# A hybrid-mixer and mixture-of-experts trunk: queue order in the merge, tile-by-tile second half of the last projection, 2 MB expert loads and piecewise contraction waits

## The reference

```python
xn = rms_norm(h, norm1_g)
h = h + hybrid_mixer(xn, ...)          # four branches of width 256, then:
    branch = einsum('bskw,kwd->bskd', ys, branch_w)
    gates = sigmoid(xn @ merge_gate_w + merge_gate_b).reshape(bn, s, 4, 1024)
    merged = sum(gates * branch, axis=2)
    return merged @ w_out
xn = rms_norm(h, norm2_g)
h = h + hier_moe(xn, ...)              # 4 groups x 8 experts, top-1 group, top-2 experts:
    h_e = silu(xb @ w1[e]) * (xb @ w3[e])     # w1, w3: 1024 x 512
    y_e = h_e @ w2[e]                         # w2: 512 x 1024
return rms_norm(h, final_norm_g)
```

## Time and profile before

| | |
|---|---|
| median of 3 runs | 2709.32 us (2708.64 to 2713.03) |
| profiled execution, its own time | 2708.18 us |
| its span | 2706.5 us |
| PE busy | 2394.8 us, 88% of the span |
| DVE, ACT, POOL busy | 1365.7, 1102.4, 656.5 us |
| merge | about 556 to 1716.5 us of the span |
| route | 1716.5 to about 1770 us |
| experts | about 1770 to 2650 us |

### The profile page before, as it was taken

One profiled execution on the slowest core, in us unless ns is written; L12 is line 12 of the kernel. 1 busy time (PEld: TensorE's weight loads), 2 busy tenths in 40 slices (PEclk: granted clock), 3 DMA queues, 4 the chain that ended last, 5 costly groups with the idle time before them and its releaser, 6 DMA issues. The chain is left out here.

```text
span 2706.5 us, 33463 instructions
## 1 busy us (share of the span) xinstructions
PE 2394.8 (88%) x11388; PEld 1875.1 (69%) x11389; DVE 1365.7 (50%) x1922; ACT 1102.4 (41%) x1380; POOL 656.5 (24%) x515
## 2 busy tenths in 40 slices
PE   6679679789989999899989999489999999999890
PEld 5567567568868888788878888366666666677670
DVE  6768464544444344434434443645555554556554
ACT  4423324123333333233323332246566665567653
POOL 4811001000000000000000000076555656547660
PEclk9889889899999999999999999689999999999995
DMA  8753546434354334533353332369878977889877
GB/s 252 272 193 126 210 147 230 128 87 128 97 177 138 119 98 148 171 125 97 113 177 114 97 99 91 146 225 302 276 240 271 306 260 259 263 285 346 287 258 271
DMA packets 360507, 516.29 MB, mean 191 GB/s; under 512 B 32668, under 2 KB 211104, under 8 KB 360416
## 3 DMA queue, kind: packets, MB, share of 16 engines
q1 hardware_dynamic: 343952, 458.17, 49.5%
q0 software_dynamic: 16464, 56.90, 8.3%
HBM read 430.33 MB, written 84.68 MB: 190 GB/s over the span
## 5 line engine op out<-in xcount | busy, mean ns | idle before, releaser
L1468 PE MATMUL mrgps<-xn_hi,w_hi 128*128 128x512 f32 x1024 | 402.3, 393 | 9.5 <-DVE w_lo L1566 9.5
L1468 PE MATMUL mrgps<-xn_lo,w_hi 128*128 128x512 f32 x1024 | 400.2, 391 | 0.0
L1468 PE MATMUL mrgps<-xn_hi,w_lo 128*128 128x512 f32 x1024 | 400.1, 391 | 0.0
L1902 POOL TENSOR_TENSOR w_lo<-w_raw,w_hi 128x1024 fp32r<-128x1024 f32 x128 | 326.4, 2753 | 0.4 <-ACT w_hi L1893 0.4
L1409 ACT ACTIVATE gt<-mrgps,mb 128x512 f32<-128x512 f32 x128 | 88.3, 690 | 505.7 <-PE mrgps L1468 505.7
L1704 POOL IOTA io_g<- 128x4 f32 x1 | 0.1, 144 | 1156.3 <-POOLq L1218 1156.3
L1897 DVE TENSOR_TENSOR w_lo<-w_raw,w_hi 128x2048 fp32r<-128x2048 f32 x125 | 280.5, 2304 | 0.1
L1582 DVE SCALAR_TENSOR_TENSOR tmp<-gt,mrgps 128x512 f32<-128x512 f32 x96 | 66.0, 688 | 389.4 <-PE mrgps L1468 389.4
L1888 ACT ACTIVATE w_hi<-w_raw 128x2048 fp32r<-128x2048 f32 x128 | 240.0, 1914 | 16.5 <-DMA w_raw<-in_expert_w_dram 16.4
L686 PE MATMUL mixps<-xn_hi,win_hi 128*128 128x512 f32 x448 | 187.4, 418 | 65.8 <-DVE xn_lo L864 22.6
L1468 PEld LDWEIGHTS mrgps<-xn_hi,w_hi 128*128 128x128 f32 x1024 | 193.3, 189 | 51.3 <-issue 8.1
(11 more groups left out here) (414 smaller groups left out, 4397.6 us busy)
## 6 DMA issues: line engine op xcount, KB each, us to landing
w_raw<-in_expert_w_dram SPq DMA_DIRECT2D x128, 1024.0 KB, 9.7
w_raw<-in_merge_gate_w_dram SPq DMA_DIRECT2D x128, 512.0 KB, 4.0
w_raw<-in_expert_w_dram SPq DMA_DIRECT2D x32, 2048.0 KB, 13.7
win_hi<-w_in_parts SPq DMA_DIRECT2D x42, 512.0 KB, 3.7
win_lo<-w_in_parts SPq DMA_DIRECT2D x42, 512.0 KB, 5.2
w_raw<-in_branch_w_dram SPq DMA_DIRECT2D x128, 128.0 KB, 4.1
wout<-in_w_out_dram SPq DMA_DIRECT2D x64, 256.0 KB, 3.6
w_raw<-in_x_dram SPq DMA_DIRECT2D x16, 512.0 KB, 10.2
```

The costliest lines, as they stand in the source:

```text
L1468: last = pe.matmul(bank[:], w[:, u % 2, kk], x, start=(kk == w_tiles[0] and j == 0), stop=(kk == w_tiles[-1] and j == 2))
L1902: eng.tensor_tensor(self.lo2[:, f], self.raw2[:, f], self.hi2[:, f].bitcast(F32), ALU.subtract).then_inc(self.split2, 1)
```

## The change

In the merge, SP issues pieces 4 and 5 of `w_out` inside the last unit, and deals the four transfers of the next input and the four of the residual rows out between pieces 6 to 11. In the last trip, the second column half is computed tile by tile (`project_tile`): all eight pieces for one tile of tokens, then the next tile. For that the eight split pieces must be there together; they are put where the normalised input stood (`wout_parts`), which nobody reads any more. Residual, square, scale, norm, turn and router product follow tile by tile, between the projections of later tiles; turning and routing use the PSUM banks of the units (`turn_banks`). In the experts, w1 and w3 come in one transfer of 2 MB each; a partition holds eight consecutive rows of the weight (16 KB in one stretch) instead of rows 128 apart, and `turn_x` takes every eighth channel of a gathered row to match. ACT writes one quarter before the turned rows and three after them. The contraction waits for w2's pieces one by one, and for each pair of pieces runs the products with the high part of the turned rows first (these wait for ACT only), then those with the low part.

```diff
+        def wout_parts(m, n):
+            if m == TRIPS - 1 and n >= KD:
+                return x_hi[:, n - KD], x_lo[:, n - KD]
+            q = m * NWO + n
+            return wo_hi[:, q % PARTS], wo_lo[:, q % PARTS]
+
+        def turn_banks(m):
+            return (gbank, bbank) if m == TRIPS - 1 else (tbank, rbank)
...
+                    if i == UNITS - 1:
+                        load_wout(m, RAWS + 1)
+                        load_wout(m, RAWS + 2)
-                if m + 1 < TRIPS:
-                    load_x_parts(m + 1)
-                for n in range(RAWS + 1, RAWS + 3):
-                    load_wout(m, n)
-                load_rows(m)
                 for n in range(RAWS + 3, NWO):
                     load_wout(m, n)
-            store_h(TRIPS - 1)
+                    if m + 1 < TRIPS and n in (6, 7, 10, 11):
+                        load_x_part(m + 1, *divmod((6, 7, 10, 11).index(n), 2))
+                    if n in (8, 9):
+                        load_rows(m, range(2 * (n - 8), 2 * (n - 8) + 2))
             for t in range(MT):
+                store_h(TRIPS - 1, (t,))
                 store_xn(TRIPS - 1, t)
...
+            m = TRIPS - 1          # ACT
+            for t in range(MT + 2):
+                if t < MT:
+                    square(m, t)
+                if t >= 2:
+                    logitsT(m, t - 2)
+                if 1 <= t <= MT:
+                    turn(m, t - 1)
...
+            def project_tile(m, t):
+                pe.wait_ge(o_free, 2 * MT * m + t + 1)
+                rows = slice(t * P, (t + 1) * P)
+                for kk in range(KD):
+                    if t == 0:
+                        pe.wait_ge(wo_split, m * NWO + KD + kk + 1)
+                    hi, lo = wout_parts(m, KD + kk)
+                    for j, (x, w) in enumerate(((mg_hi, hi), (mg_hi, lo), (mg_lo, hi))):
+                        last = pe.matmul(obank[t][:], x[:, kk, rows], w, start=(kk + j == 0), stop=(kk == KD - 1 and j == 2))
+                last.then_inc(o_full, 1)
...
+            m = TRIPS - 1          # DVE
             for t in range(MT):
+                residual(m, 1, t)
+                scales(m, t, 1)
+                norm(m, t)
+                if t == MT - 1:
+                    logit(m, 0)
+            for t in range(1, MT):
+                logit(m, t)
...
-    def load13(self, eng, e, i):
-        name, q = ("expert_w1", "expert_w3")[i // 2], KD * P // 2 * (i % 2)
-        src = self.io[name][0, ds(e, 1), q:q + KD * P // 2, :].rearrange("o (k p) n -> p (o k) n", p=P)
-        eng.dma_start(self.raw13[:, i].rearrange("p (k n) -> p k n", n=DE), src).then_inc(self.in13[i], 16)
+    def load13(self, eng, e, w):
+        src = self.io[("expert_w1", "expert_w3")[w]][0, ds(e, 1)].rearrange("o (p k) n -> p (o k) n", k=KD)
+        eng.dma_start(self.raw13[:, 2 * w:2 * w + 2].rearrange("p i (k n) -> p (i k) n", n=DE), src).then_inc(self.in13[w], 16)
...
-                for i in range(4):
-                    sp.wait_ge(wt.split13, e * 4 + (i + 1))
-                    if i == 0:
+                for w in range(2):
+                    sp.wait_ge(wt.split13, e * 4 + (2 * w + 2))
+                    if w == 0:
...
-                    last = pe.transpose(tbank[h][:, k * P:(k + 1) * P], xg[:, (4 * h + k) * P:(4 * h + k + 1) * P], ident[:])
+                    last = pe.transpose(tbank[h][:, k * P:(k + 1) * P], xg[:].rearrange("p (c k) -> p k c", k=KD)[:, 4 * h + k], ident[:])
...
-            def contract(g, f):
-                if f % 2 == 0:
-                    pe.wait_ge(h_split, g * 2 + (f // 2 + 2))
-                for c in range(2):
...
+            def contract(g, e4):
+                for j in range(2):
+                    two = (2 * j, 2 * j + 1)
+                    pe.wait_ge(h_high, g * 2 + (j + 2))
+                    for f in two:
+                        pe.wait_ge(wt.split2, e4 + (f + 1))
+                        for c in range(2):
+                            if f == 0:
+                                pe.wait_ge(y_free, g * 2 + (c + 2))
+                            for i, weights in enumerate((wt.hi2, wt.lo2)):
+                                pe.matmul(ybank[c][:], h_hi[:, f], weights[:, f, c * 512:(c + 1) * 512], start=(f + i == 0), stop=False)
+                    pe.wait_ge(h_split, g * 2 + (j + 2))
+                    for c in range(2):
+                        for f in two:
+                            last = pe.matmul(ybank[c][:], h_lo[:, f], wt.hi2[:, f, c * 512:(c + 1) * 512], start=False, stop=(f == FE - 1))
+                        if j == 1:
+                            last.then_inc(y_ps, 1)
...
-                pe.wait_ge(wt.split2, e4 + 4)
-                for f in range(FE):
-                    contract(g, f)
+                contract(g, e4)
```

137 lines of the change are left out of this document (71 added, 66 removed).

## The result

The changed kernel takes 2672.9 us (median of 5 runs) against 2712.5 us of the kernel before: a ratio of 0.9866, 95% interval 0.9851 to 0.9882. By the ratio that is 36 us faster (40 by the two medians) where 79 were forecast, and the time lies 8 us above the range's upper end. The sign was right, the size wrong by half or more.

A forecast was written before the change was run, and what follows sets the result against it. PE, busy 88% of the span, was taken to set the end. Merge 39 + tail 8.6 + experts 32 (14.4 + 35.2 - 17.6) = 79.6 us off 2708.2, forecast 2630 us; 2612 to 2646 within this case, 2610 to 2665 overall (0.8).

The forecast's parts named there:

- The merge, trips 0 to 2: Output projection: w_out pieces and residual rows arrive in time, PE's stalls in three trips go; 39 us gained, 40.7 at most.
- The tail: Merge's trip 3, last projection to route: chain of 10.7 instead of 26.1 us, less added costs; net 8.6 us gained.
- The contraction's order: Experts: contraction starts on ACT's hT_hi, not DVE's hT_lo; 0.45 us in each of 32 blocks, 14.4 us gained.
- The waits by piece: Experts' contraction waits for w2 piece by piece: excess waits of 22.4 and slow clock of 12.8 go, 35.2 us gained.
- What is late next: Experts: DMA limit 5, first expert 2.5, late 2 MB loads 6.3, one late block 3.8; 17.6 us not gained.
- The turned rows: Experts' turn of x: strided weight load on PE taken to cost nothing; upper bound 27 us over 50 blocks.
- The long stretches: Experts' weight loads: fewer packets save some 0.4 us per expert, 5 us in all at most; left out of the sum.
- the coarse load holds ACT: Rival, experts: 15 quarters 1.1 us late, each with low clock; 38 us lost, experts give nothing, 2662 us; chance 0.12.

The follow-up runs named there:

- after: The changed kernel, profiled in a second set of runs (r1) against the kernel before: 2676.88 us, ratio 0.9865.
- r2: The kernel before with only SP's new queue order in the merge: ratio 0.9848 to the kernel before.
- r3: The kernel before with the whole new merge, experts untouched: ratio 0.9823 to the kernel before.
- r5: The new merge plus, of the experts' edits, only the contraction (order and waits by piece): ratio 0.9834 to the kernel before.
- r10: New merge, new contraction, 8 KB stretches in four 1 MB transfers with strided turn, w2 in four 512 KB transfers: 0.9662 of the kernel before.
- r13: r10 with the contraction of before: ratio 0.9798 to the kernel before.
- r9: The changed kernel with w2 in four 512 KB transfers, each requested when its own quarter is split: ratio 0.9756 to the kernel before.
- r6: New merge, new contraction, 8 KB stretches in four 1 MB transfers with strided turn, w2 whole: ratio 0.983 to the kernel before.
- r1: The changed kernel run once more for a profile at the ordinary clock: 2676.88 us, ratio 0.9865 to the kernel before.
- r11: The changed kernel with ACT's old order, two quarters of w1 written before the turned rows: ratio 0.989 to the kernel before.

## Why the prediction was wrong, point by point

- **The merge, trips 0 to 2: right.** 39 forecast; 36.8 in the trace of after, 34.9 of them in the trips, 41 by r2 (0.9822 to 0.9874, so 34 to 48). What is left is one stop of PE at half time of each trip, for DVE's residual behind a late piece.
- **The tail: right in mechanism, 2.6 us too good.** 6.0 in the trace instead of 8.6; the router product in front of the last turn was taken at 1.94 us without a wait, and stood 2.55 and then took 3.18. r3 less r2 is 0.0025, 7 us, within the spread of both.
- **"The contraction's order", 32 x 0.45 = 14.4: the step is right, and it was kept only in part.** PE's wait before the contraction after a half block fell from 0.59 to 0.08 us. A stretch with a half block that follows another fell from 31.8 to 31.4 us in r5, but in the changed kernel to 31.7 only. What the singles won came back as a wait in the half block behind them.
- **"The waits by piece", 35.2: here the forecast failed.** PE's waits for w_lo went from 28.4 to under 1 us as said, and the 35.2 us were booked as gained. The text then asked "what is late next" and tried the bytes and the first quarter of w1, not the buffer of w2 itself, whose landing it took at nothing. The cycle was to be read in the earlier trace rows with one row of SP more: 20.8 us against 18.7. What PE won in the singles came back as a wait for hg in the next half block: 14.1 gained, 26.9 lost. With w2 whole the contraction's two edits gave nothing (r5 against r3, 0.9834 and 0.9823); with w2 in pieces the same edits give 37 us (r10 against r13).
- **"What is late next", 17.6: the coarse transfers were undersized.** 6.3 us were counted for them, beside 5 for the bytes, 2.5 for the first expert and 3.8 for one block that was late already. r10 against r9 puts them at 25 us with the cycle open, r6 against r1 at 9 (0.983 against 0.9865) with it closed. The sum looked at the first quarter only, one split late and in 7 experts; ACT's waits for w1 and w3 grew from 16.4 us before to 60.1 in after, and behind each of them stands everything else in ACT's queue.
- **The turned rows: taken at nothing, and nothing it is.** The load itself grew by 51 ns, near the upper bound. The bound was right, and the argument for zero (the load isn't held by the rate of reading) was wrong: the load does get longer with the stride, but it overlaps the loads and transpositions beside it, whose starts stay 109 to 111 ns apart. That the result is right is luck in this step. The Trainium skill (SBUF — State Buffer, "Door 1: The DMA port swizzle") says that each new line costs, beyond a stride of about four float32; the trace agrees with it in the duration of the load (141 to 192 ns), and shows next to nothing of it in the pace of the transpositions.
- **The long stretches: left out, and worth 15 us once w2 comes in pieces.** The forecast left them out. With w2 in pieces, 2 KB instead of 8 KB stretches cost 0.0055 of the time, 15 us; with 2 MB transfers and w2 whole, 2 KB instead of 16 KB cost 0.007, 19 us; with 1 MB transfers and w2 whole, nothing. The packets in the traces have the price: one of 2, 4, 8 and 16 KB takes 84, 159, 309 and 611 ns, that is 9 ns for each beside 75 ns for each 2 KB. For the 4 MB of w1 and w3 on 16 DMA engines, 8 KB instead of 2 KB then save an estimated 0.9 us per expert, some 27 us in 31, of which 15 came through. The Trainium skill (DMA: Bandwidth & Descriptors, "Why small descriptors are slow (HBM only)") has about 3 extra cycles per packet, from which the forecast's estimate was 0.4 us per expert and 5 us at most; the direction holds, but 9 ns on 75 are 12% and not the 4.5% of that estimate. Wrong too was to count it only where the DMA engines are the bound: it also counts where a landing holds a loop.
- **The rivals.** That of 2662, "the coarse load holds ACT", had the right culprit for part of the loss, and its time was 11 us off; but it looked for the loss in ACT's turned rows, and it stands at the tanh of the half block. Its nearness to the result is luck in part, since it knows nothing of w2. No rival named w2's cycle.
- **The range** ended at 2665 because none of its cases let the experts lose. The lower end of "waits by piece" should have been nothing gained; r5 against r3 shows just that, and the coarse transfers then cost on top.

Open: in the changed kernel the gains of pieces (0.9756) and of the moved write (0.9755) are known one by one, not together. That 2 MB transfers cost 25 us even with w2 in pieces is shown as an effect (r9 against r10; r11 excludes ACT's order only for w2 whole); that it goes through ACT's waits for w1 and w3 is read from the waits (69.5 against 28.2 us) and not tested by a run. Nor was the strided turn run without the long stretches.
